# A last layer that opens with both value projections inside the MLP's last product

## The reference, cut to what matters

```
x = first_block(x, ...)              # mixers, then the MLP: x = x + relu(h2 @ w_up)**2 @ w_down
h = rms_norm_2(x, pre_norm_gain)     # the last layer, 512 tokens by 1024 features
q, kv, g, z = split_cols(h @ w_in, [1024, 6 * 256, 48, 3 * 1024])
k_c, v_c, k_s, v_s, k_w, v_w = split(kv)
kc = silu(windows(k_c) @ k_w1) @ k_w2            # compressed keys, 31 windows; vc likewise
o_cmp = softmax(q kc + bias) vc
o_slc = softmax(q k_s + bias) v_s                # here all blocks are taken
o_win = softmax(q k_w + bias) v_w
x + rms_norm_2((gates * (o_cmp, o_slc, o_win) * silu(z)).sum @ w_out, post_norm_gain)
```

## Time and profile before

| what | value |
|---|---|
| median of 3 runs | 1359.02 us (1358.73 to 1359.62) |
| the profiled execution | 1358.28 us, of which the span is 1356.6 us |
| PE busy | 1314.5 us, 97% of the span |
| DVE, ACT, POOL busy | 763.5, 679.5, 201.7 us |

### The profile page before, as it was taken

The page is one execution under the profiler, slowest core; times in us unless marked ns, Lnnn a source line. Parts: engine busy times, 40 slices in busy tenths (PEclk is TensorE's granted clock), DMA queues, the critical chain, the costliest instruction groups (busy, mean ns, idle before and its releaser), DMA issues.

```text
span 1356.6 us, 17827 instructions
## 1 busy us (share of the span) xinstructions
PE 1314.5 (97%) x7149; PEld 1098.8 (81%) x7149; DVE 763.5 (56%) x1217; ACT 679.5 (50%) x1053; POOL 201.7 (15%) x265
## 2 busy tenths in 40 slices
PE   6999999999999999999999999899999999999998
PEld 4887777787788887878878787788899998989876
DVE  4753444434544544595775858721266767776563
ACT  5244555347666424454635546445245667665232
POOL 1101332261000000000000000003612333331000
PEclk9999999999999999999999999999999999999999
DMA  8657443394435334134070420372612222222311
GB/s 172 103 121 115 73 85 70 88 205 113 62 63 62 81 106 159 59 114 135 1 236 12 154 95 1 93 221 78 139 38 72 71 71 71 69 94 66 108 63 62
DMA packets 94817, 128.97 MB, mean 95 GB/s; under 512 B 5839, under 2 KB 70463, under 8 KB 94736
## 3 DMA queue, kind: packets, MB, share of 16 engines
q1 hardware_dynamic: 88528, 108.70, 31.9%
q0 software_dynamic: 6064, 18.83, 5.3%
q10 hardware_dynamic: 144, 0.31, 0.1%
HBM read 124.94 MB, written 2.88 MB: 94 GB/s over the span
## 4 chain that ended last, share of the span: by engine, by line
PE 86%; DVE 7%; ACT 3%; DMA 2%; issue 2%; SPq 0%; POOL 0%; DVEq 0%; ACTq 0%
PE ps_g L633 44%; PE ps_g L656 8%; PE ps_z L656 8%; PE ps_t L1277 6%; PE ps_z L1388 3%; PE ps_z L1425 2%; PE ps_z L1277 2%; PE ps_t L1460 2%; DVE w_lo L610 2%; DMA w_raw<-in_w_in 2%; PE ps_t L1155 1%; ACT w_hi L602 1%; PE ps_t L1193 1%; PE ps_z L1207 1%; PE ps_t L1310 1%
## 5 line engine op out<-in xcount | busy, mean ns | idle before, releaser
L610 DVE TENSOR_TENSOR w_lo<-w_raw,w_hi 128x2048 fp32r<-128x2048 f32 (+1 forms) x84 | 193.5, 2304 | 233.0 <-ACT w_hi L602 233.0
L633 PE MATMUL ps_g<-act_hi,w_hi 128*128 128x512 f32 x784 | 310.3, 396 | 6.4 <-DVE act_lo L754 4.3
L633 PE MATMUL ps_g<-act_hi,w_lo 128*128 128x512 f32 x784 | 306.7, 391 | 0.0
L633 PE MATMUL ps_g<-act_lo,w_hi 128*128 128x512 f32 x784 | 306.5, 391 | 0.0
L602 ACT ACTIVATE w_hi<-w_raw 128x2048 fp32r<-128x2048 f32 (+1 forms) x84 | 159.2, 1895 | 113.3 <-PE ps_g L656 62.1
L633 PEld LDWEIGHTS ps_g<-act_hi,w_hi 128*128 128x128 f32 x784 | 148.0, 189 | 39.3 <-issue 5.0
L633 PEld LDWEIGHTS ps_g<-act_hi,w_lo 128*128 128x128 f32 x784 | 148.0, 189 | 31.5
L633 PEld LDWEIGHTS ps_g<-act_lo,w_hi 128*128 128x128 f32 x784 | 148.1, 189 | 29.7
L633 PE MATMUL ps_g<-w_hi,act_hi 128*128 128x256 f32 x320 | 93.4, 292 | 0.0
L633 PE MATMUL ps_g<-w_lo,act_hi 128*128 128x256 f32 x320 | 90.3, 282 | 0.0
L633 PE MATMUL ps_g<-w_hi,act_lo 128*128 128x256 f32 x320 | 90.2, 282 | 0.0
(11 more groups left out here) (349 smaller groups left out, 2602.0 us busy)
## 6 DMA issues: line engine op xcount, KB each, us to landing
w_raw<-in_w_in SPq DMA_DIRECT2D x32, 1024.0 KB, 9.2
w_raw<-in_nsa_w_in SPq DMA_DIRECT2D x22, 1024.0 KB, 5.2
w_raw<-in_w_up SPq DMA_DIRECT2D x16, 1024.0 KB, 5.6
down_raw<-in_w_down SPq DMA_DIRECT2D x16, 1024.0 KB, 5.2
tile_t<-bias_rev_dram POOLq DMA_DIRECT2D x32, 256.0 KB, 3.1
bc<-stat_rows_dram POOLq DMA_DIRECT2D x24, 256.0 KB, 10.2
w_raw<-in_w_out SPq DMA_DIRECT2D x4, 1024.0 KB, 5.0
w_raw<-in_nsa_w_out SPq DMA_DIRECT2D x4, 1024.0 KB, 5.0
```

Of the source, the lines that this page charges most:

```text
L610: nc.vector.tensor_tensor(slab_view(w_lo[b], n), slab_view(raw(n), n), slab_view(w_hi[b], n).bitcast(F32), ALU.subtract).then_inc(lo_done, 1)
L633: mm = nc.tensor.matmul(o, stationary, moving, start=(k == 0 and j == 0), stop=(k == KT - 1 and j == 2))
```

## The change

The values' two slabs become one wide pair `N_V`, `N_V+1` (columns of both values, 512 together; each half holds half of the contraction), first in the layer. Every token block gets its own root, `xn` carries the gain (loaded once as `pre_bc`, 4 KB for each partition), and PE takes the transposes of block 0 between the two tiles of M4 and those of block `b+1` inside the wide matmuls of block `b`. ACT and DVE handle half a block (four feature tiles of 128 tokens) at a time. `N_KC`, `N_VC`, `N_NG` follow, then the query slabs with the two compressions between them; the tiles of `N_KS` and `N_KW` now lie between the steps of the compressed attention. The diff, cut:

```diff
-        vs = sb("vs", [P, TB, 256], at=arena + K16 + 8192)
-        vw = sb("vw", [P, TB, 256], at=arena + K16 + 12288)
+        vsw = sb("vsw", [P, 2, TB, 256], at=arena + K16 + 8192)
+        pre_bc = sb("pre_bc", [P, D], at=arena + 5 * K16 + 12288)
...
-        N_NQ = add("nq", NW, NQ, 4)
+        N_V = add_wide("nv", NW, NVS, 1)
         N_KC = add("nkc", NW, NKC, 1)
         N_VC = add("nvc", NW, NVC, 1)
         N_NG = add("ng", NW, NG, 1, w=P)
+        N_NQ = add("nq", NW, NQ, 4)
         N_KS = add("nks", NW, NKS, 1)
         N_KW = add("nkw", NW, NKW, 1)
-        N_VS = add("nvs", NW, NVS, 1)
-        N_VW = add("nvw", NW, NVW, 1)
         N_NZ = len(slabs)
...
-        CMP_TILES = (((N_VS, 2),), ((N_VS, 3), (N_VW, 0)), ((N_VW, 1),), ((N_VW, 2), (N_VW, 3)))
+        CMP_TILES = ((N_KS, 1, 0, KT), (N_KW, 0, 0, KT), (N_KW, 1, 0, HALF_K), (N_KW, 1, HALF_K, KT))
...
-        NORM_PARTS = (((0, 1), (1, 3), (3, 4)), ((0, 3), (3, 4)), ((0, 3), (3, 4)))
+        NORM_PARTS = (((0, 1), (1, 3), (3, 4)), ((0, 3), (3, 4)), ((0, 1), (1, 2), (2, 3), (3, 4)))
...
+                if slabs[n][4] == "nv":
+                    for e, at in enumerate((NVS, NVW)):
+                        src = mat[row0:row0 + HALF_K * P, at:at + 256].rearrange("(k p) n -> p k n", p=P)
+                        sp.dma_start(slab_view(w_raw[b], n)[:, :, 256 * e:256 * e + 256], src)\
+                            .then_inc(raw_landed[b], 16)
+                    return
...
+            sp.wait_ge(prod_added, added(3, M1, 1))
+            sp.dma_start(pre_bc[:], a["pre_g"].rearrange("a b -> (a b)").partition_broadcast(P)).then_inc(pre_in, 16)
+            for n in range(N_V, N_ALL):
+                if n == N_NG:
+                    sp.wait_ge(second_t, 2 * TB)
                     for dst, name in ((w1k, "nsa_cmp_k_w1"), (w1v, "nsa_cmp_v_w1")):
                         sp.dma_start(dst[:], a[name].rearrange("(k p) n -> p k n", p=P))\
                             .then_inc(w1_in, 16)
...
+            def second_turns(b):
+                pe.wait_ge(xn_ready, 2 * TB + b + 1)
+                for j in range(2):
+                    if b == 0:
+                        pe.wait_ge(prod_added, added(3, M3, 1))
+                    elif b == 1:
+                        pe.wait_ge(prod_added, added(3, M4, 1))
+                    else:
+                        pe.wait_ge(second_lo, 2 * (b - 2) + j + 1)
+                    for k in range(4):
+                        mm = nc.tensor.transpose(second_bank(b, j)[:, k * P:(k + 1) * P],
+                                                 xn[b][:, (4 * j + k) * P:(4 * j + k + 1) * P], ident)
+                    mm.then_inc(second_t, 1)
+            down_product(3, M4, (0,))
+            second_turns(0)
+            down_product(3, M4, (1,))
+            pe.wait_ge(lo_done, N_V + 1)
+            wh, wl = slab_view(w_hi[N_V % 2], N_V), slab_view(w_lo[N_V % 2], N_V)
+            for b in range(TB):
+                t, m = tile_of[N_V] + b, slice(b * P, (b + 1) * P)
+                wait_bank(pe, t)
+                pe.wait_ge(second_hi, 2 * b + 1)
+                for k in range(HALF_K):
+                    nc.tensor.matmul(bank(t), act_hi[:, k, m], wh[:, k, :], start=(k == 0), stop=False)
+                    nc.tensor.matmul(bank(t), act_hi[:, k, m], wl[:, k, :], start=False, stop=False)
+                    if k == 0:
+                        pe.wait_ge(second_lo, 2 * b + 1)
+                    mm = nc.tensor.matmul(bank(t), act_lo[:, k, m], wh[:, k, :], start=False, stop=False)
+                    if k == 2 and b < TB - 1:
+                        second_turns(b + 1)
+            mm.then_inc(half_done, 1)
+            for b in range(TB):
+                pe.wait_ge(second_lo, 2 * b + 2)
+                mm_half(pe, N_V + 1, b)
+            for n in (N_KC, N_VC, N_NG, N_NQ):
+                mm_slab(pe, n)
             def compress(which, w1):
@@ -1319,8 +1363,9 @@
...
-            mm_tile(pe, N_KW, 0)
+            mm_slab(pe, N_NQ + 1)
             pe.wait_ge(hid_ready, 1)
+            wait_tile_free(pe, tile_of[N_V])
...
+            mm_slab(pe, N_NQ + 2)
+            pe.wait_ge(hid_ready, 2)
+            pe.wait_ge(hid_pad, 1)
...
+            mm_slab(pe, N_NQ + 3)
...
+            mm_tile(pe, N_KS, 0, ks=range(HALF_K))
             cmp_scores(0)
...
+            mm_tile(pe, N_KS, 0, ks=range(HALF_K, KT))
             for b in range(TB):
                 cmp_transposes(b)
                 if b < TB - 1:
                     cmp_scores(b + 1)
-                for n, i in CMP_TILES[b]:
-                    if (n, i) == (N_VW, 3):
-                        scores(0)
-                    mm_tile(pe, n, i)
+                else:
+                    scores(0)
+                n, i, k0, k1 = CMP_TILES[b]
+                mm_tile(pe, n, i, ks=range(k0, k1))
...
+            def second_squares(b):
+                act.wait_ge(prod_added, added(3, (M3, M4)[b // 2], b % 2))
+                nc.scalar.activation(xn[b][:], x_sb[:, b, :], ACT.Square,
+                                     accum_out=ssq[:, 2, b:b + 1]).then_inc(sq_done, 1)
+            def second_root(b):
+                act.wait_ge(var_ready, parts_before(2) + b + 1)
+                nc.scalar.activation(rstd[:, 2, b:b + 1], ssq[:, 2, b:b + 1], ACT.Sqrt).then_inc(std_ready, 1)
+            def second_high(b, j):
+                act.wait_ge(second_t, 2 * b + j + 1)
+                nc.scalar.copy(second_blocks(act_hi, b, j), second_bank(b, j).rearrange("p (k t) -> p k t", t=P))\
+                    .then_inc(second_hi, 1)
+            nc.scalar.activation(rstd[:, 2, 0:1], ssq[:, 1, 0:1], ACT.Sqrt).then_inc(table_asked, 1)
+            act.wait_ge(table_asked, 1)
+            second_squares(0)
+            second_root(0)
+            split_hi(act, N_V)
+            second_squares(1)
+            second_root(1)
+            second_high(0, 0)
+            second_high(0, 1)
+            second_squares(2)
+            split_hi(act, N_V + 1)
+            second_root(2)
+            second_high(1, 0)
+            second_high(1, 1)
+            second_squares(3)
+            second_root(3)
+            for b in (2, 3):
+                for j in range(2):
+                    second_high(b, j)
             def hidden(which):
                 act.wait_ge(hid_mm, which + 1)
...
+            def second_mean(b):
+                dve.wait_ge(sq_done, parts_before(2) + b + 1)
+                v = ssq[:, 2, b:b + 1]
+                nc.vector.tensor_scalar(v, v, 1.0 / D, EPS, ALU.mult, ALU.add).then_inc(var_ready, 1)
+            def second_normed(b):
+                dve.wait_ge(std_ready, parts_before(2) + b + 1)
+                r = rstd[:, 2, b:b + 1]
+                order.link(nc.vector.reciprocal(r, r))
+                if b == 0:
+                    dve.wait_ge(pre_in, 16)
+                nc.vector.scalar_tensor_tensor(xn[b][:], x_sb[:, b, :], r, pre_bc[:], ALU.mult, ALU.mult)\
+                    .then_inc(xn_ready, 1)
+            def second_low(b, j):
+                dve.wait_ge(second_hi, 2 * b + j + 1)
+                nc.vector.tensor_tensor(second_blocks(act_lo, b, j),
+                                        second_bank(b, j).rearrange("p (k t) -> p k t", t=P),
+                                        second_blocks(act_hi, b, j).bitcast(F32), ALU.subtract).then_inc(second_lo, 1)
+            add_product(3, M3, 0)
+            second_mean(0)
+            second_normed(0)
+            add_product(3, M3, 1)
+            split_lo(dve, N_V)
+            second_mean(1)
+            second_low(0, 0)
+            add_product(3, M4, 0)
+            second_normed(1)
+            second_low(0, 1)
+            second_mean(2)
+            add_product(3, M4, 1)
+            second_low(1, 0)
+            second_normed(2)
+            second_mean(3)
+            second_low(1, 1)
+            second_low(2, 0)
+            second_normed(3)
+            split_lo(dve, N_V + 1)
+            second_low(2, 1)
+            second_low(3, 0)
+            second_low(3, 1)
+            nc.vector.memset(hid_v[:, :, :, :, NCMP:CPAD], 0.0).then_inc(hid_pad, 1)
+            for n in range(N_V + 1, N_NQ):
                 split_lo(dve, n + 1)
-            nc.vector.memset(hid_v[:, :, :, :, NCMP:CPAD], 0.0).then_inc(hid_pad, 1)
-
+            split_lo(dve, N_NQ + 1)
...
+            split_lo(dve, N_KS)
...
+            split_lo(dve, N_KW)
             cmp_logits(0)
```

More of the change, by code:

```diff
@@ L675, in feature_bank, with feature_tiles @@
             return (ps_z, ps_t)[k // 3][:, k % 3 * 512:(k % 3 + 1) * 512]
-        def feature_tiles(pe, n, src, block_ready, between=None, before=None, late=None):
+        def feature_tiles(pe, n, src, block_ready, between=None, before=None):
             t0 = norm_tile_of[n]
@@ L694, in feature_tiles @@
                     wait_tile_free(pe, tile_of[before] + 1)
[L695 to L704, removed]
+                turn(j, range(2, KT))
             if between is not None:
```

(33 more changed lines are left out.)

99 lines of the change are left out of this document (44 added, 55 removed).

## The result

The changed kernel takes 1361.04 us in the median (1359.32 to 1363.86, 20 runs), the kernel before 1358.57 beside it: ratio 1.002, 95% interval 1.0014 to 1.0026. It is slower by 2.5 us. The profiled execution has 1359.44, of which 1357.7 are the span.

What follows compares the result with a forecast made beforehand. PE, busy 97% of the span, was taken to bound the kernel with its list and waits. +19.95 - 23.4 + 0.5 + 1.6 + 1.3 = -0.05 us gave 1358.2 profiled, 1358.9 median; eight-in-ten range 1354.6 to 1362.6.

Steps and rivals of the forecast that it cites:

- The opening: From M4's second tile's old start to the first N_KC matmul: 31.7 us, so what follows starts 19.95 later.
- its 0.75, 1.35 and 1.1: PE's predicted waits in us: at block 0's transposes, at block 1's, and in block 3 behind act_lo.
- that rival: PE's clock falls after the waits of 1.35 and 1.1, costing 3.3 us: 1362.2; chance 0.12, two thirds of it slower.
- the two later waits: PE waits in the compressed attention: +1.6 us at the first block's logit transposes, +1.3 at scores(0).
- the tiles that went: Eight tiles of 24 matmuls with 256 columns each leave PE's list: -23.4 us.
- the returns: Returns to matmuls because N_KS and N_KW tiles come in five pieces and the queries are cut: +0.5 us.
- the five waits: PE's new waits: 0.75, 1.35 and 1.1 us with the wide values, then 1.6 and 1.3 in the compressed attention.
- The steps of 122 and 227 ns: Time between successive PE matmuls of 256 and 512 columns; by them the widening saves 1.5 us.
- the prediction's other figure, 1360.3: Forecast if PE matmuls followed the skill's N / 2.4 plus 2.5 ns, so that widening saved 0.2 us, not 1.5.
- the sum: Whole kernel: +19.95 - 23.4 + 0.5 + 1.6 + 1.3 = -0.05 us against 1358.28, so 1358.2 for a profiled execution.
- What I cost at nothing: Items priced at zero: the gates-slab w_lo wait, value and compression-weight loads, w_hi of N_KC, POOL's compression inputs, ACT's additional root.
- The step from the profiled execution to the median: Whole kernel: the profiled execution lies 0.74 us below the median, so the median after is 1358.9.

Runs made afterwards that it cites:

- the two pairs of profiles: Changed kernel and kernel before, first as measured, then both run again unchanged: 1360.51 (ratio 1.0014) and 1357.76 us (0.9996).
- early loads: Either kernel with tile_t (bias) loads asked for sooner on POOL; medians over three pairs: 1356.3 us for the kernel before, 1357.4 for the changed one.
- all reordered: Changed kernel with six reorderings of its adds, w_lo, logits and matmuls, tile_t loads left as they are: 1355.99 us, ratio 0.9990.
- the first edit on POOL: Either kernel with load_bias ahead of q_lo, every fourth load still behind key_lo: kernel before 1356.23 us, changed kernel 1357.23.

## Why the prediction was wrong

**The opening** came out as walked: 31.66 us for 31.7. The rows give its waits as 0.70, 1.07 and 0.88, counted from the end of the matmul before; counted as the prediction does, from the moment at which the next matmul could have started, they are 0.86, 1.23 and 1.04 for its 0.75, 1.35 and 1.1. The clock stayed at 1.00, and that rival is out. In the same way the two later waits are 1.61 for 1.6 and 1.27 for 1.3. With **the tiles that went** and the returns they leave the region at +0.03 in the first pair of profiles and +0.22 in the second, for the -0.05 forecast. This was no luck: each of the five waits was there at its price, and reordering took four of them down by most of it. The steps of 122 and 227 ns held as well (0.12 and 0.23 us between rows of the changed kernel too). The section "Back-to-back issue gap" of the Trainium skill's page "TensorE: Matmul & The Clock Gate" gives N / 2.4 + 2.5 for a single matmul on its own and not for a stream with weight loads, so the prediction's other figure, 1360.3, had no ground in it.

**The step that failed is the sum**: "-0.05 us against 1358.28, so 1358.2 for a profiled execution". It takes over the 1358.28 with everything in it that lies behind the region, the loop of 221.64 included, as if a region that ends at the same moment left the rest alone. "What I cost at nothing" does not name the loop, and no rival let unchanged code become slower. The sum has nothing for it where the two pairs of profiles have 2.1 and 2.9 us: the loop measured 223.76 and 223.58, for 221.64 and 220.72 before. That it is the late bias loads is shown by the early ones, which make the loops equal (219.90 and 220.03); that the place of PE's instruction loads decides how many are late is shown by the kernel before with 72 idle instructions, which becomes 1.5 us slower and stalls at the changed kernel's loads. How much of the gap in spans this is: by what early loads took from it, 1.9 of 2.7 over all runs, or 1.2 of 2.0 on the one chip.

**The other 0.8** stays open. No profiled pair with early loads shows it (spans 1355.7, 1354.3, 1356.2 before, 1354.4, 1354.5, 1355.1 changed): the first part of the program, the same in both kernels, ends anywhere from 862.45 to 865.20 at M3's add, and the changed kernel's first profiles happened to lie at the low end, so a single pair can hide or feign a microsecond. Region, loop and the time behind the loop (102.4 in every profile) are level, so the profiles do not show where the other executions of the changed kernel lose it. **The step from the profiled execution to the median** (0.74 added) was for this reason no more than chance: the changed kernel's median is 1.6 over its profiled execution.

The size that decided was also missed for a second reason: the prediction priced the waits that the new order brings at 2.9 and 3.2, and took them as given. Against the version without most of them, they are the difference between this change and one that is faster with the loop as it is (0.9990, interval 0.9981 to 0.9999; 2.0 us in the median).

## What to carry to other kernels

When a change adds or removes instructions on a long engine list, the later instruction loads move against the later small transfers, as the 72 idle instructions showed. A transfer with less slack than such a load can take from it (here up to two microseconds) is then a stall that comes and goes with edits elsewhere. Give such transfers their slack first (here one line moved on POOL, 1.4 to 1.9 us of the kernel before), and compare changes of a few tenths of a per cent only afterwards. And when a wait is priced in a prediction, ask in the same line which instruction could stand in its place.

## What was unexpected of the hardware

- One 16 KB packet of instructions delays a 256 KB load that is under way from 3.0 to as much as 5.2 us (changed kernel, all reordered: packet 1.60 us after the request). The many small packets of a 1 MB slab load did not: in the two profiles with the first edit on POOL, 13 bias loads had 230 to 380 KB of a slab moving beside them and no packet of instructions, and landed after 3.0 to 3.5. Most of the late loads, in turn, had no slab beside them.
- Some small DVE instructions are several times longer beside an instruction of POOL: of the 28 `rneg` that overlap one in the changed kernel, 22 took 0.17 us and six 0.32 to 0.90; of the four such multiplies of `rgate`, three took 1.02 to 1.14, this one beside POOL's `k_lo`:

```profile
1128.98 0.17 DVE L2196 RECIPROCAL rgate<-rsum 128x4 f32<-128x4 f32 x1
1129.19 1.02 DVE L2197 TENSOR_TENSOR rgate<-rgate,gates_n 128x4 f32<-128x4 f32 x1
```

  (changed kernel with early loads, DVE's timeline). In every loop three of these multiplies are this long, and 1.5 to 1.8 us behind each stands one of the three stalls of 1.1 us that `o_b`, which reads `rgate`, ends. That the one makes the other was not tested; no run here removed them.
- An instruction that only waits, for two semaphores that have long come, costs PE 0.106 us from start to start: 72 of them, 7.7 us, more than filled a wait of 2.16.
